# A ring of weight slots and its activations at other byte offsets in on-chip memory

## The reference, cut to what matters

```
h = rms_norm(x, g_mix);  ... = split(h @ w_in)          # 2048 x 6160
x = x + concat([attn, ssm]) @ w_out                      # 2048 x 2048
x = x + cross_attention(rms_norm(x), rms_norm(mem), ...) # w_cq, w_ckv, w_co
x = x + square(relu(rms_norm(x) @ w_up)) @ w_down        # 2048 x 8192 x 2048
h = x @ w_in_2                                           # 2048 x 12368
x = layer_norm(a * x + merged @ w_out_2)
u = causal_dwconv(x @ w_up_2); f = (silu(gate) * up) @ w_down_2   # 2048 x 11264, 5632 x 2048
out = layer_norm(a * x + f)
```

## The kernel before, in words

| start modulo 512 | before |
|---|---|
| WH, slots 0, 1, 2, 3 | 96, 112, 128, 160 |
| WL, slots 0, 1, 2, 3 | 160, 176, 192, 224 |
| XH and XL | 224 and 224 |
| AH and AL | 424 and 488 |
| MH and ML | 420 and 484 |

## Time and profile before

### The profile page before, as it was taken

One profiled execution on the slowest core, in us unless ns is written; L12 is line 12 of the kernel. 1 busy time (PEld: TensorE's weight loads), 2 busy tenths in 40 slices (PEclk: granted clock), 3 DMA queues, 4 the chain that ended last, 5 costly groups with the idle time before them and its releaser, 6 DMA issues.

```text
span 2831.4 us, 52761 instructions
## 1 busy us (share of the span) xinstructions
PE 2776.3 (98%) x22440; PEld 2715.0 (96%) x22440; DVE 1788.2 (63%) x2601; ACT 1341.0 (47%) x1811; POOL 110.7 (4%) x75
## 2 busy tenths in 40 slices
PE   8999999999999999999999999999899999999997
PEld 8998899899999999999899999999899999999996
DVE  6787679675555555555676786456576546654666
ACT  5464566454344343444344774444454434443543
POOL 2000021010000000000000000000400000000003
PEclk9999999999999999999999999999899999999998
DMA  6533445455555555555444555555365555555552
GB/s 235 171 136 136 157 142 178 135 199 182 186 186 180 185 187 182 184 185 174 142 164 144 170 174 185 186 185 165 120 199 184 184 184 186 186 183 183 186 186 83
DMA packets 136604, 488.45 MB, mean 173 GB/s; under 512 B 15153, under 2 KB 17585, under 8 KB 136369
## 3 DMA queue, kind: packets, MB, share of 16 engines
q1 hardware_dynamic: 136368, 485.09, 50.8%
HBM read 482.93 MB, written 2.10 MB: 171 GB/s over the span
## 4 chain that ended last, share of the span: by engine, by line
PE 97%; DVE 1%; issue 1%; ACT 1%; DMA 0%; SPq 0%; ACTq 0%; DVEq 0%
PE ps L753 96%; PE ps L756 1%; DVE T L1694 0%; DMA cst<-in_cst 0%; ACT xT L1177 0%; DVE small L1702 0%; DVE q L1694 0%; DVE small L1694 0%; ACT P L1177 0%; DVE P L1698 0%; SPq L706 0%; ACT T L1177 0%; SPq L709 0%; DVE WL L1694 0%; ACT WH L1177 0%
## 5 line engine op out<-in xcount | busy, mean ns | idle before, releaser
L1694 DVE TENSOR_TENSOR WL<-raw,WH 128x1024 fp32r<-128x1024 f32 x907 | 1120.2, 1237 | 860.1 <-ACT WH L1177 857.4
L1177 ACT ACTIVATE WH<-raw 128x1024 fp32r<-128x1024 f32 x907 | 961.1, 1060 | 1420.1 <-PE ps L753 1419.0
L753 PE MATMUL ps<-XH,WH 128*128 128x256 f32 x5024 | 1425.5, 284 | 23.6 <-issue 10.8
L753 PE MATMUL ps<-XH,WL 128*128 128x256 f32 x5024 | 1418.8, 282 | 0.0
L753 PE MATMUL ps<-XL,WH 128*128 128x256 f32 x5024 | 1414.4, 282 | 0.0
L753 PEld LDWEIGHTS ps<-XH,WH 128*128 128x128 f32 x5024 | 947.8, 189 | 31.4 <-issue 27.3
L753 PEld LDWEIGHTS ps<-XL,WH 128*128 128x128 f32 x5024 | 946.8, 188 | 2.3 <-issue 1.5
L753 PEld LDWEIGHTS ps<-XH,WL 128*128 128x128 f32 x5024 | 946.7, 188 | 0.3
L753 PE MATMUL ps<-AL,WH 128*128 128x256 f32 x1856 | 526.1, 283 | 0.0
L753 PE MATMUL ps<-AH,WH 128*128 128x256 f32 x1856 | 525.0, 283 | 0.2 <-DVE AL L1694 0.2
L753 PE MATMUL ps<-AH,WL 128*128 128x256 f32 x1856 | 524.7, 283 | 0.0
(11 more groups left out here) (227 smaller groups left out, 1644.0 us busy)
## 6 DMA issues: line engine op xcount, KB each, us to landing
raw<-in_w_up SPq DMA_DIRECT2D x304, 512.0 KB, 3.5
raw<-in_w_in SPq DMA_DIRECT2D x224, 512.0 KB, 3.4
raw<-in_w_down SPq DMA_DIRECT2D x216, 512.0 KB, 3.4
raw<-in_w_out SPq DMA_DIRECT2D x64, 512.0 KB, 3.4
raw<-in_w_gates SPq DMA_DIRECT2D x64, 512.0 KB, 3.5
raw<-in_w_ckv SPq DMA_DIRECT2D x16, 512.0 KB, 3.2
raw<-in_w_cq SPq DMA_DIRECT2D x8, 512.0 KB, 3.9
raw<-in_w_co SPq DMA_DIRECT2D x8, 512.0 KB, 3.3
```

Source lines behind the costliest of these rows:

```text
L753: return e.matmul(out, l, r, start=start, stop=True, skip_group_check=True)
L1177: return e.activation(out, x, func, **kw)
L1694: return e.tensor_tensor(out, a, b, op)
```

## The change

Only start addresses change. The slots get SKEW (0, 32, 64, 96) elements, so slot s begins s x (4096 + 128) bytes behind the start of `WH` or `WL`. Each tensor that has a skew is padded by 128 elements instead of 16. `XH` and `XL` become skewed tensors too, with a skip of 16 elements; A gets 16 instead of 10, M 96 instead of 9.

```diff
-SKEW = (0, 4, 8, 16)
+SKEW = (0, 32, 64, 96)
...
         def skewed(name, n, skip, stack):
 
-            return sb(name, [128, n * 256 + 16], F32R, stack)[:, skip:skip + n * 256].rearrange("p (a t) -> p a t", t=256)
+            return sb(name, [128, n * 256 + 128], F32R, stack)[:, skip:skip + n * 256].rearrange("p (a t) -> p a t", t=256)
...
-        WH = sb("WH", [128, RING * GRAN + 16], F32R)
-        WL = sb("WL", [128, RING * GRAN + 16], F32R)
-        XH = sb("XH", [128, 16, 256], F32R)
-        XL = sb("XL", [128, 16, 256], F32R)
+        WH = sb("WH", [128, RING * GRAN + 128], F32R)
+        WL = sb("WL", [128, RING * GRAN + 128], F32R)
+        XH = skewed("XH", 16, 16, ctx)
+        XL = skewed("XL", 16, 16, ctx)
...
-                MH = skewed("MH", 8, 9, p1c)
-                ML = skewed("ML", 8, 9, p1c)
+                MH = skewed("MH", 8, 96, p1c)
+                ML = skewed("ML", 8, 96, p1c)
...
-            AH2 = skewed("AH2", 16, 10, p2)
-            AL2 = skewed("AL2", 16, 10, p2)
+            AH2 = skewed("AH2", 16, 16, p2)
+            AL2 = skewed("AL2", 16, 16, p2)
...
-            AH4 = skewed("AH4", 16, 10, p4)
-            AL4 = skewed("AL4", 16, 10, p4)
+            AH4 = skewed("AH4", 16, 16, p4)
+            AL4 = skewed("AL4", 16, 16, p4)
```

## The result

| | before | after |
|---|---|---|
| median, us | 2834.68 | 2762.53 (2762.11 to 2762.95, 2 runs) |
| ratio | 1 | 0.9745, 95% interval 0.9704 to 0.9787 |
| span of the profiled execution, us | 2831.4 | 2760.3 |
| PE matmul busy, us | 2776.3 | 2704.7 |
| DVE, ACT busy, us | 1788.2, 1341.0 | 1788.5, 1339.7 |

The kernel became 2.6% faster. The median, 2762.53, lies under the range of 2770 to 2880, and beyond the 2% that the prediction had thought unlikely.

The account below looks back on a forecast made before the run. PE bounds the kernel through matmul pitch. Span 2831.4 - 10.6 (X) - 1.1 (A) = 2819.7 us, with the median 3.3 above it, about 2823; own range 2810 to 2835, 8 in 10 range 2770 to 2880.

Parts of the forecast that it names:

- What bounds it: Whole kernel: PE is the bound, time is matmul count times pitch, and operand byte offsets are worth a few nanoseconds per matmul.
- (3): M and moving-weight jobs, 768 matmuls, 1.2 us either way; small float32 matmuls, 1.7 us; both taken as 0.
- (4): ACT and DVE writing WH and WL at other offsets: any growth covered by 1419.0 and 857.4 us of waiting, so nothing.
- Step (1): Matmuls with X moving: all distances 0 modulo 64, so every slot at 117.7 ns instead of 118.4, gain 10.6 us.
- Step (2): Matmuls with A moving: all distances 32 modulo 64, so 120.0 ns instead of 120.2, gain 1.1 us.
- (a): Rival, 20%: A also gains because its start becomes a multiple of 16, reaching 117.7 ns, 13 us more, 2810.
- (b): Rival, 8%: the change does nothing; the pitch remainder goes with slot number by chance, time 2835.
- (c): Rival, 14% in full or part: one shared bad distance costs one X matmul in three 0.02 us, 100 us, 2935.
- (d): Rival, 18% in full or part: reads cease to meet, X and A fall to "dt"'s 113.5 ns, 111 us, 2724.

Follow-up runs that it names:

- e3: Changed kernel with X, A and M begun at distances 0, 16 and 48 bytes modulo 128 from the weights: 2833.5 us (one run).
- e7: Changed kernel with A and M placed like X and WL's slots 64 bytes further on, so one load in three is at distance 0: 2814.4 us (one run).
- e1: Changed kernel with A and M begun at the same place as X, distance 64 modulo 128 from the weights: 2730.8 us, ratio to before 0.9634.
- e8: Changed kernel with A and M placed like X, then all weights, X, A and M 8 bytes further on, distances kept at 64: 2869.9 us, ratio 1.0121.
- e9: Changed kernel with X, A and M begun 68, 72 and 56 bytes modulo 128 from the weights: 2854.4 us (one run).
- e11: Changed kernel with A and M placed like X, then all weights, X, A and M 16 bytes further on: 2734.3 us, ratio 0.9645.
- e4: Changed kernel with A and M placed like X, then weights, X, A and M all 32 bytes further on, distances kept at 64: 2729.6 us, ratio 0.9631.
- e10: Changed kernel with A and M placed like X and weight slots alternating between places 96 and 224 modulo 512: 2730.8 us, ratio 0.9634.
- e6: Changed kernel with A and M placed like X and no stagger, all weight slots at 96 modulo 512: 2781.0 us, ratio 0.9838.
- e12: Changed kernel with A and M placed like X and weight slots alternating between places 96 and 352 modulo 512: 2780.7 us, ratio 0.9808.
- e2: Changed kernel with the slots' old skews (0, 4, 8, 16) put back, X distances 64, 48, 32, 0: 2795.9 us, ratio 0.9861.

## Why the prediction was wrong, point by point

**What bounds it.** Right. PE stayed the bound, the pitch was the whole matter, ACT and DVE were covered, and (3) and (4) cost nothing to be seen.

**Step (1), X.** Here it failed. The step said that the distance counts modulo 64, from four points, and so gave all slots the pitch of slots 0 and 3, 117.7 ns. It measured 113.3. The sum gave it a gain of 10.6 us. The chunks give 77, and 65 are left of the 71 by which the span fell when A's 6 are taken off. In slots 0 and 3 of before WH and WL stood at different distances, 0 for the one and 64 for the other. e3 shows 0 alone (119.2), the changed kernel 64 alone (113.3), e7 the mixture made on purpose (118.1). The 117.7 was the price of a mixture and was read as the price of both parts. The last paragraph of the prediction named this gap, 0 and 64 modulo 128 mixed in slots 0 and 3, and gave it no price.

**Step (2), A.** Forecast 120.0 ns, measured 119.2. The size was off by 0.8 ns, 4.5 us, and the slots were not equal (120.0 and 118.3). e1 shows what the distance held back: 32 us, with M.

**(a), the lines.** A start off a multiple of 16 does cost: at distance 64 A runs at 113.3 ns aligned (e1) and at 120.6 ns 8 bytes off (e8). A did not fall to 117.7 by its alignment, since at its new distances it stays slow: e1 differs from the changed kernel in the places of A and M alone and has A at 113.3 against 119.2 ns. The Trainium skill, "SBUF — State Buffer", Specifications, with its 16-byte lines, agrees with e8 and e9 in kind; 16 bytes on (e11) still costs a little, which it does not say.

**(b), nothing happens.** Refuted: between e1 and e3 only the places of X, A and M move, X by 64 bytes, and X chunks take 21.76 and 22.88 us. The Trainium skill, "TensorE: Matmul & The Clock Gate", Part 2, has the load take nothing from the running matmul. The runs disagree, by up to 6 ns in 113.

**(c), slower by one shared distance.** Not for 64. With 0 shared by all X matmuls the time is that of before and no more (e3, 2833.5 us). Its price was also misread. The 0.14 us of the earlier trace rows stands once in a granule: over the steady slot-2 granules of that trace the second matmul takes 134 ns in the mean, and the seven others of its kind 117 to 122. The prediction charged it to one matmul in three.

**(d), the reads cease to meet.** X fell to the number of this case, the pitch of "dt"; that it is the reads which cease to meet is a picture that no run shows. It had 18%. What I held against it, that the distance sweeps 512 bytes in every matmul whatever it is at the start, may be true and decides nothing. The row of "dt" said how much there was to win and was used only as a bound: four slots at 117.5 to 120.0 show only that none of eight distances in mixtures is good, not that no distance is.

**The range.** Its lower end was halfway into (d), 2779, widened a little to 2770. In the chunks X went all the way and A hardly moved; X alone at "dt"'s pitch is 74 us in the prediction's own bounds, 2835 - 74 = 2761.

**What stays open.** Why a distance of 64 or 192 modulo 256 is fast and the ten others measured are not; what puts a stream into the slow steady pitch, and whether the step of 128 bytes or the place at 192 takes it out. The runs show where it is fast and not why. Distances that are not a multiple of 16 were tried only together with a misaligned operand.

## What to carry to other kernels

All this was measured for one shape: float32r, 128x128 weight tiles loaded anew for each matmul, 256 moving columns. Where long weight loads run beside every matmul, compare the pitch with a stretch whose loads are short: here the difference was what the placing of operands could win (118.4 against 113.5 ns). Put both operands at multiples of 32 bytes, with 64 bytes modulo 128 between every moving tile and every weight tile, high and low parts alike, and let successive buffers differ by 128 bytes modulo 256, as e1, e4 and e10 do. When several places are mixed in one measurement, do not give the mixture's value to its parts; make each alone.

## What the runs showed of the hardware that I had not expected

One pair of operand places has two steady pitches, 113.3 and 117.8 ns, and a stream keeps the one it is in for a chunk of 192 matmuls (e6, e12) and for thousands (e6: 6024 and 5616). "dt", with 16-column loads, is slower in these two kernels as well, 5.62 against 5.44 us. With starts at multiples of 16, and apart from that slow pitch, one pitch goes with each distance modulo 256, and 64 and 192 are the good ones of twelve (e2, e3 and the changed kernel). One load in three at a bad distance costs four fifths of what all three cost (e7: 4.7 of 5.8 ns). A moving start 4 bytes off a multiple of 16 costs 6.9 ns per matmul of 256 columns with short loads (e9, "dt" 5.77 against 5.44 us), 3.1 of them beyond the slow "dt" of e6.
